# Nineteen block pairs in an mLSTM and convolution trunk: three heads' keys, values and queries as pairs through DRAM, one mLSTM step for every column piece

## What is computed

```
xn = rmsnorm(x);  q,k,v,o,i,f,u,g = split(xn @ w_in)      # 1024 -> 4096+8+2048+2048 channels
A: per head (4 heads of 256), chunk after chunk:
   s = (q k^T) * w;  num = s v + inter * q C;  h = num / max(|den|, floor)
   C = decay * C + k^T (w v)                               # carried to the next chunk
   ya = (rmsnorm(h) * sigmoid(o)) @ w_proj_a
B: glu = u[:D] * sigmoid(u[D:]);  c = causal depthwise conv, width 31
   yb = silu(layernorm(c)) @ w_proj_b
x = x + rmsnorm((sigmoid(gA) ya + sigmoid(gB) yb) @ w_out)
x = x + rmsnorm(down(gelu(conv3(up gate)) * conv3(up value)))   # 1024 -> 2 x 2816 -> 1024
```

## Time and profile before

| | us |
|---|---|
| median of 3 runs (lowest, highest) | 1934.39 (1932.95, 1935.28) |
| the profiled execution | 1933.08 |
| its span in the trace | 1931.2 |
| PE busy | 1905.2 (99%) |
| DVE busy | 1295.2 (67%) |
| ACT busy | 832.2 (43%) |

### The profile page before, as it was taken

How to read it: one execution, slowest core, us unless ns; L and a number is a source line. 1 busy time by engine, 2 the same in 40 slices (tenths; PEclk the granted TensorE clock), 3 DMA queues, 4 the chain that set the end, 5 groups by cost and what they waited for, 6 DMA issues and landing times.

```text
span 1931.2 us, 32359 instructions
## 1 busy us (share of the span) xinstructions
PE 1905.2 (99%) x13095; PEld 1881.5 (97%) x13095; DVE 1295.2 (67%) x1991; ACT 832.2 (43%) x1534; POOL 69.5 (4%) x122
## 2 busy tenths in 40 slices
PE   9999999999999999999999999999999999999997
PEld 8999999999999999899999999999999999999997
DVE  7798989696777735354444468977677677646363
ACT  5454444423333334463122345654445444545342
POOL 0000000011111111110000000000000000000000
PEclk9999999999999999999999999999999999999998
DMA  3323222444343347658231313212122122556554
GB/s 133 129 82 130 101 97 86 159 121 101 85 123 95 96 114 215 178 179 311 94 137 44 129 53 126 87 71 79 69 89 79 68 88 91 201 189 216 205 175 153
DMA packets 108675, 240.24 MB, mean 124 GB/s; under 512 B 19052, under 2 KB 58732, under 8 KB 108528
## 3 DMA queue, kind: packets, MB, share of 16 engines
q1 hardware_dynamic: 99600, 205.66, 31.0%
q0 software_dynamic: 8928, 32.51, 7.4%
HBM read 182.20 MB, written 55.94 MB: 123 GB/s over the span
## 4 chain that ended last, share of the span: by engine, by line
PE 91%; DVE 4%; DMA 2%; ACT 1%; issue 1%; SPq 0%; POOL 0%; DVEq 0%; ACTq 0%; POOLq 0%
PE ps L1069 12%; PE ps L1070 12%; PE ps L1071 12%; PE ps L1428 7%; PE ps L1426 7%; PE ps L1427 7%; PE ps L1226 4%; PE ps L1227 4%; PE ps L1228 4%; PE ps L1444 4%; PE ps L1445 4%; PE ps L1446 4%; PE ps L1158 2%; PE ps L1155 1%; PE ps L1138 1%
## 5 line engine op out<-in xcount | busy, mean ns | idle before, releaser
L1069 PE MATMUL ps<-rx,fhi 128*128 128x364 f32 (+2 forms) x1120 | 376.1, 336 | 3.0 <-DMA flo<-wts 2.4
L1070 PE MATMUL ps<-rx,fhi 128*128 128x364 f32 (+2 forms) x1120 | 364.8, 326 | 0.0
L1071 PE MATMUL ps<-rx,flo 128*128 128x364 f32 (+2 forms) x1120 | 364.6, 326 | 0.0
L1069 PEld LDWEIGHTS ps<-rx,fhi 128*128 128x128 f32 x1120 | 211.3, 189 | 5.3 <-issue 2.9
L1070 PEld LDWEIGHTS ps<-rx,fhi 128*128 128x128 f32 x1120 | 211.3, 189 | 1.5
L1071 PEld LDWEIGHTS ps<-rx,flo 128*128 128x128 f32 x1120 | 211.1, 188 | 0.0
L1444 PE MATMUL ps<-ghi,dhi 128*128 128x384 f32 (+1 forms) x528 | 173.2, 328 | 2.7 <-DVE glo L2723 2.3
L1445 PE MATMUL ps<-glo,dhi 128*128 128x384 f32 (+1 forms) x528 | 172.3, 326 | 0.0
L1446 PE MATMUL ps<-ghi,dlo 128*128 128x384 f32 (+1 forms) x528 | 172.2, 326 | 0.0
L2716 DVE TENSOR_TENSOR dlo<-draw,dhi 128x1408 fp32r<-128x1408 f32 x48 | 77.7, 1624 | 118.7 <-ACT dhi L1975 118.6
L1590 ACT ACTIVATE qkv<-ps 128x364 f32<-128x364 f32 (+1 forms) x72 | 34.0, 473 | 202.2 <-PE ps L1071 202.1
(11 more groups left out here) (345 smaller groups left out, 5330.1 us busy)
## 6 DMA issues: line engine op xcount, KB each, us to landing
draw<-wdn SPq DMA_DIRECT2D x48, 704.0 KB, 4.2
uraw<-wts SPq DMA_DIRECT2D x44, 512.0 KB, 4.3
fhi<-wts POOLq DMA_DIRECT2D x31, 512.0 KB, 7.0
flo<-wts POOLq DMA_DIRECT2D x31, 512.0 KB, 6.2
fraw<-wts SPq DMA_DIRECT2D x27, 512.0 KB, 3.6
araw<-wts SPq DMA_DIRECT2D x52, 256.0 KB, 2.6
scr_g<-cva SPq DMA_DIRECT2D x22, 512.0 KB, 2.6
graw<-scr_g SPq DMA_DIRECT2D x43, 192.0 KB, 4.1
```

Source lines behind the costliest of these rows:

```text
L1069: pe.matmul(b, hi[:, w], src[:, his[k], cols], start=(k == 0), stop=False)
L1070: pe.matmul(b, hi[:, w], src[:, los[k], cols], start=False, stop=False)
L1071: mm = pe.matmul(b, lo[:, w], src[:, his[k], cols], start=False, stop=(k == KB - 1))
```

## The change

The six tiles of keys, values and queries of each of heads 1, 2 and 3 leave the plain part and become nine pairs, and the tiles ga and gb of gate blocks 4, 5 and 6 leave the pairs and become plain (those of block 7 are plain already). There are then 19 pairs and 12 plain tiles fewer. The pairs' results for the heads are stored to a new DRAM tensor scr_qkv and come back in `load_head`, six loads of 544 KB for a head: head 1 at piece 20, head 2 behind the last step of head 0 and head 3 behind the last of head 1. Each step now begins one piece after the last (`STEP_AT` = S_B + 22 + i), so a piece holds the scores of step i, the values of step i - 1 and the rows of step i - 3. The scores move from the end of the piece on PE into its middle, their PSUM bank from 4 to 3, and on ACT ahead of the piece's evacuation. The convolution's operations are handed out anew (12 in the first pair and 14 in each later one, in place of 6 and 13; then 26 pieces in place of 64), and so are the layer norm's sums and passes. Constants and the order of weights follow.

```diff
-            + [("gate", 0)] + head(0, "kvq") + head(1, "kvq") + head(2, "kvq") + head(3, "kvq")
-            + [("ga", 7), ("gb", 7)] + one("o", 1, KB))
+            + [("gate", 0)] + head(0, "kvq")
+            + [(kind, m) for m in range(4, KB) for kind in ("ga", "gb")] + one("o", 1, KB))
-PAIRS_B = [("u", 2), ("g", 0), ("g", 1), ("u", 3), ("g", 2), ("u", 4), ("g", 3), ("u", 5), ("g", 4), ("u", 6), ("g", 5),
-           ("u", 7), ("g", 6)]
+PAIRS_B = [("u", 2), ("k", 1), ("v", 1), ("u", 3), ("q", 1), ("k", 2), ("u", 4), ("v", 2), ("q", 2), ("u", 5), ("k", 3),
+           ("v", 3), ("g", 0), ("u", 6), ("q", 3), ("g", 1), ("u", 7), ("g", 2), ("g", 3)]
-SUM_AFTER = {S_B + 66: ("mu", 0), S_B + 67: ("mu", 1), S_B + 70: ("mu", 2),
+SUM_AFTER = {S_B + 27: ("mu", 0), S_B + 28: ("mu", 1), S_B + 29: ("mu", 2),
-STEP_AT = [S_B + 22 + 2 * i for i in range(len(STEPS))]
+STEP_AT = [S_B + 22 + i for i in range(len(STEPS))]
-TAPS_AT = [6] + [12 + 13 * i for i in range(NB)]
+TAPS_AT = [6] + [18 + 14 * i for i in range(NB)]
-for r_ in range(64):
+for r_ in range(26):
     left_ = NOP * KB - TAPS_SLOT[-1]
-    TAPS_SLOT.append(TAPS_SLOT[-1] + (2 if r_ < 10 else 5 if r_ < 22 else left_ // (64 - r_)))
+    TAPS_SLOT.append(TAPS_SLOT[-1] + (2 if r_ < 4 else -(-left_ // (26 - r_))))
-PASS1 = {FULL[S_B + 71 + 3 * k // 2]: k for k in range(KB)}
-PASS2 = {FULL[S_B + at]: k for k, at in enumerate((88, 89, 91, 92, 94, 96, 97, 99))}
+PASS1 = {FULL[S_B + 31 + 2 * k]: k for k in range(KB)}
+PASS2 = {FULL[S_B + at]: k for k, at in enumerate((52, 53, 54, 56, 57, 61, 62, 63))}
...
+            def load_head(h):
+                if h == 1:
+                    for x in range(2):
+                        sp.wait_ge(spl_out[x], 16 * V0_STORES[x][NB])
+                    sp.wait_ge(v1_out, 16 * V1_STORES[NB])
+                    sp.wait_ge(gt_set, 4)
+                    sp.wait_ge(gate_dve, 16)
+                else:
+                    sp.wait_ge(qk_in, 96 * (h - 1))
+                    sp.wait_ge(nq_full, NSTEP * (h - 1))
+                for b in range(6):
+                    sp.dma_start(qkv[h % 2][:, b, :], scr_qkv[h - 1, b]).then_inc(qk_in, 16)
...
+                i = step_at(s, 2)
+                if s == GATE_END + 18:
+                    load_head(1)
+                if i is not None and STEPS[i][1] == NSTEP - 1 and STEPS[i][0] < 2:
+                    load_head(STEPS[i][0] + 2)
...
                 if i:
                     pe.wait_ge(kv_copied, 2 * i)
                     pe.wait_ge(a_set, i)
-                    pe.wait_ge(hn_set, i)
+                if rows_before(i):
+                    pe.wait_ge(zs_set, 2 * rows_before(i))
...
             def rows_out(i):
                 pe.wait_ge(zt_set, i + 1)
+                pe.wait_ge(a_set, scores_before(i))
...
-                    rows, halfway = None, None
+                    i = step_at(s, 0)
+                    rows, halfway = None, (lambda: scores(i)) if i is not None else None
```

More of the change, by code:

```diff
@@ L88 @@
 ORDER_B = ((1, 0), (1, 1), (5, 0), (5, 1), (6, 0), (6, 1), (2, 0), (7, 0), (7, 1), (2, 1), (4, 0), (4, 1), (3, 0), (3, 1))
-G_BEFORE = [sum(kind == "g" for kind, _ in PAIRS_B[:i]) for i in range(NB + 1)]
-U_BEFORE = [i - G_BEFORE[i] for i in range(NB + 1)]
-SPL_AT = [1 + 2 * i + G_BEFORE[i] for i in range(NB + 1)]
+U_BEFORE = [sum(kind == "u" for kind, _ in PAIRS_B[:i]) for i in range(NB + 1)]
+V1_STORES = [i - U_BEFORE[i] for i in range(NB + 1)]
+SPL_OF = {"u": (0, 2), "g": (1, 2), "k": (1, 1), "v": (0, 0), "q": (0, 0)}
+SPL_AT = [1 + sum(sum(SPL_OF[kind]) for kind, _ in PAIRS_B[:i]) for i in range(NB + 1)]
 V0_STORES = [[1 - p + len(range(p, min(i, NB), 2)) for i in range(NB + 2)] for p in range(2)]
@@ L179, in step_at, with rows_before, scores_before @@
     return STEP_IN.get(NTH_FULL[s] - after)
+def rows_before(i):
+    return sum(at + 3 < STEP_AT[i] for at in STEP_AT)
+def scores_before(i):
+    return sum(at <= STEP_AT[i] + 3 for at in STEP_AT)
 def step_cols(j):
     return slice(j * L, (j + 1) * L) if j < NCHUNK else slice(T - L, T)
-TAPS_AT = [6] + [12 + 13 * i for i in range(NB)]
+TAPS_AT = [6] + [18 + 14 * i for i in range(NB)]
 TAPS_SLOT = [TAPS_AT[NB]]
-for r_ in range(64):
+for r_ in range(26):
     left_ = NOP * KB - TAPS_SLOT[-1]
-    TAPS_SLOT.append(TAPS_SLOT[-1] + (2 if r_ < 10 else 5 if r_ < 22 else left_ // (64 - r_)))
+    TAPS_SLOT.append(TAPS_SLOT[-1] + (2 if r_ < 4 else -(-left_ // (26 - r_))))
 N_BY_DVE = 8
@@ L325, in build @@
     scr_u = nc.dram_tensor("scr_u", (KB, P, T), F32, kind="Internal").ap()
+    scr_qkv = nc.dram_tensor("scr_qkv", (3, 6, P, T), F32, kind="Internal").ap()
     scr_o = nc.dram_tensor("scr_o", (KB, P, T), F32, kind="Internal").ap()
@@ L703, in store_v1 @@
             def store_v1(i):
-                sp.wait_ge(spl_set, SPL_AT[i] + 2)
-                sp.dma_start(scr_gb[PAIRS_B[i][1]], v1[:, :]).then_inc(v1_out, 16)
+                kind, k = PAIRS_B[i]
+                if kind == "g":
+                    sp.wait_ge(spl_set, SPL_AT[i] + 2)
+                    to = scr_gb[k]
+                else:
+                    if kind == "k":
+                        sp.wait_ge(spl_set, SPL_AT[i] + 1)
+                    else:
+                        sp.wait_ge(c21_set, 2 * i + 2)
+                        sp.wait_ge(c22_set, 2 * i + 2)
+                    to = scr_qkv[k - 1, 2 * "kvq".index(kind) + 1]
+                sp.dma_start(to, v1[:, :]).then_inc(v1_out, 16)
             def store_v0(i):
@@ L1127, in scores @@
                     pe.wait_ge(gt_set, 4)
-                if j == 0:
+                if j == 0 and h == 0:
                     pe.wait_ge(t_free, EVAC_AT[last_slot("q", 2 * h + 1)])
+                elif j == 0:
+                    pe.wait_ge(qk_in, 96 * h)
                 if i:
@@ L1137, in scores @@
                 for b in range(2):
-                    mm = pe.matmul(bank(4, 320, L), q[:, b, cols], q[:, 4 + b, cols], start=(b == 0), stop=(b == 1))
+                    mm = pe.matmul(bank(3, 0, L), q[:, b, cols], q[:, 4 + b, cols], start=(b == 0), stop=(b == 1))
                 mm.then_inc(s_full, 1)
@@ L1287, in _ @@
                     values(i)
-                i = step_at(s, 0)
-                if i is not None:
-                    scores(i)
             pe.wait_ge(t_free, EVAC_AT[NS - 2])
@@ L1586, in evac @@
                     h = k // 2
-                    if h == 1 and kind == "k" and c == 0:
-                        act.wait_ge(neg_out, 16)
                     at = 2 * "kvq".index(kind) + k % 2
@@ L1674, in pairs @@
                     piece(i, 6, 0), piece(i, 6, 1)
-                    if i and PAIRS_B[i - 1][0] == "g":
-                        act.wait_ge(v1_out, 16 * G_BEFORE[i])
+                    if i and PAIRS_B[i - 1][0] != "u":
+                        act.wait_ge(v1_out, 16 * V1_STORES[i])
                     elif i:
@@ L1706, in _ @@
                     x_whole(3, 0), x_whole(3, 1)
+                i = step_at(s, 0)
+                if i is not None:
+                    scores(i)
                 evac(s, kind, k, c)
@@ L2852 @@
     for kind, m in PAIRS_B:
-        stream += [ga[m], gb[m]] if kind == "g" else [ua[m], ub[m]]
+        if kind in ("u", "g"):
+            stream += [ga[m], gb[m]] if kind == "g" else [ua[m], ub[m]]
+        else:
+            stream += [of[kind][2 * m], of[kind][2 * m + 1]]
     wts = np.stack(stream)
```

43 lines of the change are left out of this document (31 added, 12 removed).

## The result

| | us |
|---|---|
| before, median of 4 runs (lowest, highest) | 1933.67 (1930.58, 1935.28) |
| changed, median of 4 runs (lowest, highest) | 1974.20 (1973.92, 1974.69) |
| ratio, 95% interval | 1.0225 (1.0204 to 1.0247) |
| span of the profiled execution, before and changed | 1931.2, 1972.3 |

The change costs 2.25%. The sign was forecast, the size was not: 16.7 us more were forecast and 40.5 measured, and 1974 lies above the range's end of 1966.

What follows compares the result with a forecast made beforehand. PE, busy 99% of the span, was taken as the bound. -16.6 + 6.6 + 20.0 - 6.3 + 3.0 + 8.5 + 1.5 = +16.7 us on 1933.1 gave 1949.8, or 1951 as median; range 1937 to 1966.

Steps and rivals of the forecast that it cites:

- The sign: Whole kernel: the change makes it slower, given a chance of 0.83.
- PE's work: PE's matmuls: six pairs more at 21.20 us and twelve tiles fewer at 11.98 us, -16.6 us.
- PE's work alone: Rival: PE's wait at steps 0 to 3 vanishes and the C store is in time; 1916 us, chance 0.08.
- The first pair: First pair: six more taps on DVE make PE wait 4.8 us, not 0.55; with clock loss +6.6 us (4 to 7).
- From the pairs to step 0: Pieces 0 to 21: 36 more DVE operations delay the first exponents, debt paid by step 3's end; +20.0 us (14 to 24).
- The layer norm's passes: First pass: the 4.01 us wait for a reload goes, -6.3 us; second pass: six pieces lose a little, +3 (0 to 6).
- The C state: Head changes: late store of C delays DVE's new C and PE's values; +8.5 us (0 to 17), head 1 +1.5 (0 to 4).
- The sentence on POOL's share: C store: POOL's 1.05 MB of weight loads share the 16 engines, store 2.5 us later, time 1953.5; left out of the sum.
- The rival with the later store: Head changes: burst at 300 GB/s takes 11.1 us, C store may land in 9.4; 1961 us, chance 0.17.

Runs made afterwards that it cites:

- The version above: Changed kernel with store of C earlier, head loads one per piece, 16 taps per later pair, taps over 29 pieces, first-pass reload a piece later: 1916.17 us, ratio 0.9924.

## Why the prediction was wrong in size

**PE's work: right.** A pair is 21.18 to 21.20 us in every run, and a piece with a whole step 7.26. The version above runs 15.4 us under the kernel before (1931.54 to 1916.17). That is near the 16.6 of 6 pairs and 12 tiles, but it tests them only roughly: the kernel before has waits of 4.01 and 2.42 us that this version lacks, and this version has the 5.6 in and behind its second pass. In the same way the rival "PE's work alone" meets 1916 by luck: it counts 4.3 us for the first pair, where this version waits 0.55, and no loss in the second pass.

**The first pair: right.** 4.82 us of wait were forecast as 4.8. The pairs' stretch is 408.77 - 19 x 21.20 = 6.0 us over the plain count, of which 0.55 stood there before; taking the six taps away gave 5.8 in that stretch, against 6.6 in the sum.

**From the pairs to step 0: right.** The first exponents were forecast 107.1 us behind the start of piece 0 (461.8 - 354.7); they came at 595.42 - 488.40 = 107.0. Of DVE's two waits in that stretch the first, 4.50 us, is still there and the second is gone, as reckoned. From piece 0 to the scores of step 4 the changed kernel takes 620.89 - 488.40 = 132.5 us, and the version without stalls 593.84 - 481.66 = 112.2. The difference is 20.3, against 20.0. That the debt is DVE's is shown by the runs with more taps in the pairs: the same operations, done earlier, remove it.

**The layer norm's passes: right.** In the stretch of the two first-pass steps, 767.48 to 797.07, the kernel before spends 29.6 us on two steps, 7.1 more than 2 x 11.24, against 6.3. In the changed kernel no subtraction waits for its load, so that loss is gone. The second pass costs 3.1 us at the steps with 8.4 and 9.2 us between scores, against 3.

**The C state: wrong, and it is the whole error.** The failed step is the landing time of the store of C: "near the median, since the burst is over", 3.5 us, and for head 1 only 1.5 us in all, since it "has no first-pass wait ahead of it". The three changes of head cost 14.6, 13.8 and 4.4 us, 32.8 in place of 8.5, 1.5 and nothing, 22.8 more; the time was missed by 23.2. More than half of that is head 1, 12.3 us. Head 0's 14.6 lies within its own bounds of 0 to 17. For head 0, counted from the piece's start at 665.4 (the prediction's 13.1 and 3.5 make 16.6, where it has 16.8):
- The store of scr_xc landed at 13.0 in place of 11.5, and the store of C was issued at 14.4 in place of 13.1. This part held within 1.5 us.
- It landed in 6.6 us in place of 3.5. The burst was over for the six loads, but the reload of cs, the gate's store and POOL's 1.05 MB of weights stood in the same engines.
- Head 1's store went out 7.7 us behind the start of its own burst (15.0 at head 0), when that was not over, and took 12.5. Without a wait on SP it met more of the burst, not less. The sentence on POOL's share, which the sum left out, pointed the right way with 2.5 us and was small against what came.
- PE did not go on 0.8 us behind the landing but 2.2: the rows of the step wait, since this change, for the multiply of the newest scores, and that stands on DVE behind the copy that waits.
- I priced a burst by what it does to one transfer. Here it delayed all that were issued up to 8 us behind its start, and each had a consumer a piece or two away: with the store out of its way, the decay row was late instead and held 16.5 of the 32.8 us. Part of that, at head 0, is the wait for scr_xc on SP. The rival with the later store had this mechanism's sign, but counted the same single transfer, 10 us.
- The third change of head was not in the sum at all. There no burst is near, and the store's place alone costs 4.4 us.

## What to carry to other kernels

When a pipeline is made to run one step per piece in place of one per two, each transfer's time from issue to need is about halved too: for the decay row from some 22 us to 7 to 12 here. List every transfer that a step waits for with its slack, and put a burst of loads against all of them, not against the one that seems latest. Large loads that are not yet needed go out one at a time behind the small ones that are, and a store whose buffer is written again goes out as soon as its data is there. A sum of one engine's operations in its fixed order forecast a stall of 20 us to 0.3; a landing time taken from the median of the kernel before was off by a factor of 1.9 at one head and 3.6 at the next.

## What the runs showed of the hardware

- In one stretch a load of 64 KB landed in 3.2 us at best and in 14.7 behind six loads of 544 KB in the same queue. A store of 257 KB took 12.5 us behind such a burst, against 2.8 when it was issued ahead of it.
- Moving the burst to another engine's queue did not protect the first queue: the decay rows still took 9.2 us in the median of that stretch, in place of 13.7, and a store of C 13.3.
- A long wait can be named "issue" on the engine that shows it. The cause stood on DVE's timeline, at the copy of C, which stands ahead of the multiply that PE waited for.
- DVE bore 16 taps beside each pair without lengthening any, though one more was thought to reach the pair's 21.2 us. The room was in its waits for weights: from 105 to 480 us they are 18.1 us at 14 taps, 17 waits of up to 2.5 us, and 0.3 us at 16. DVE's busy time rose from 19.6 to 20.96 us of each 21.2.
